# A decoder trunk on one core: the next pass's gather behind the scatter, a peeled last pass, and reordered norm, gate and down-projection steps

## The chip, the cores and the metric

The program runs on one core of one Trainium2 chip. The metric is the device time of one execution in microseconds, the lower the better. All arithmetic on the path is float32.

## What is computed

Two layers work on 256 tokens of 1024 channels. Each layer normalises x, makes one input projection, runs three token mixers (gated DeltaNet, RWKV-7, stick-breaking attention), merges them by sigmoid gates, projects and adds to x. Then a second norm and a channel mixer follow, and a last norm ends the trunk. Cut to what matters here:

```python
for layer in range(DEPTH):                       # DEPTH = 2
    hn = rmsnorm(x, norm_mix_g[layer])
    proj = hn @ w_in[layer]
    ...                                          # three mixers, gates = sigmoid(h_gate)
    x = x + merged @ w_out[layer]
    hn = rmsnorm(x, norm_ffn_g[layer])
    if layer % 2 == 0: x = x + (silu(hn @ w_gate) * (hn @ w_up)) @ w_down      # 2816 hidden
    else:              x = x + moe_swiglu(hn, ...)        # top 2 of 8 experts, 3584 hidden
return rmsnorm(x, final_norm_g)
```

## The kernel before

Everything is written by hand, engine by engine: TensorE (PE), ScalarE (ACT), VectorE (DVE), GpSimd (POOL) and the queue of SyncE (SP) each have their own list of instructions, and semaphores (the `Signal` objects and plain `sem`) tie them. The order on each engine is the order in which its functions are called. The 256 tokens are two tiles of 128 (`t` = 0, 1). Weights come through a ring of slots that SP fills in the order of the `loads` list; SP waits for the release of a slot before it issues the load that follows into it.

**Norm at the start of a layer** (`scaled` L1622, `turned` L1627, called at L2037 to L2044; PE's `first_projections` L644). ACT squares a tile and makes 1/rms, DVE's `scaled` writes hn, PE transposes it, DVE's `turned` multiplies the transposed tile by the norm's weights into hnT. PE's first projections read hnT of tile 0 (L636).

**Attention** (PE L1010 to L1059, DVE L1860 to L1879, ACT's `log1p` L1524, POOL's masks L571 to L580). Eight heads go in four pairs `j`. PE makes the scores of the next pair, then some steps of other work, then the suffix sums of the pair (`sums`, L1034 and L1035), other steps, then `values` (L1045, L1048). The other steps are the first six gate projections (`gate_projections`, L623, two matmuls a step, eight steps for a gate); twelve of the 48 steps have run before attention. Two PSUM banks, `proj`, take these projections in turn, so the first matmul of gate m waits until DVE has copied gate m-2 out of its bank (`opened`, L1873, the copy is L1876). `opens` says behind which pair DVE makes which copy:

```python
opens = ((), (0, 1), (2,), (3,))
```

**Dense channel mixer of layer 0** (`dense_ffn` L1095, DVE's L1907). For each of 22 tiles of hidden channels PE makes gate and up (L1144), and one tile later the down projection (L1104), for both token tiles. The down projections of the last three tiles are kept and run token tile by token tile. DVE then adds to x (L1915), tile 0 first, and waits for both tiles before it goes on to the next layer's norm.

**Experts of layer 1** (`experts` on PE L1212, DVE L2008, ACT L1580 to L1596, SP L2145 to L2171). Tokens are sorted into passes of up to 80 slots, one expert for a pass; here 8 passes run. Each pass has four rounds; a round takes 11 MB of weights, in eight slots for gate and up and three for down. At the end of a pass PE does, in this order: `gather(i + 1)` (selection matrix times hn, L1190 with operand hn, into B[0] and B[1]), eight transposes of the pass's result (L1292), the scatter back to tokens (L1299, into B[0], B[1], proj[0], proj[1]), and `selection_rows(i + 1)` (L1207, into B[0]). ACT copies yT (L1592) and ye (L1596) between them; DVE copies the gathered tokens (`gathered`, L2000), adds the four scatter blocks to x (L2032) and copies the selection rows (L2006). The last pass does the same, though nothing follows it. Each of these loops runs a number of times that is read from a table.

**Final norm** (ACT L1598 to L1603, DVE L2053 to L2057, SP L2171 to L2174). After the loop DVE signals once (`all_added`); ACT squares both tiles and makes both 1/rms values; DVE multiplies each tile by 1/rms and the norm's weights in one SCALAR_TENSOR_TENSOR; SP stores each tile when it is done.

## Time and profile before

| | |
|---|---|
| median of 3 runs | 2057.37 us (2057.05 to 2058.26) |
| the profiled execution | 2054.16 us |
| its span, first to last instruction | 2052.4 us |
| PE busy | 1962.2 us, 96% |
| DVE, ACT, POOL busy | 392.6, 271.1, 88.2 us |
| granted TensorE clock, mean | 0.984 of full speed |
| DMA | 482.92 MB, 235 GB/s over the span |

The span leaves out what lies before the first and behind the last instruction (1.8 us of the execution's own 2054.16). PE busy counts a matmul as busy also where it runs at the lower clock. A line number names the line of the kernel; many operations of different stages share a helper's line, so stretches of time tell the stages apart. The stages of layer 0 end near 695 us, the experts begin near 1177 us.

### The profile page before, as it was taken

The numbers are of one execution on the slowest core, as the hardware profiler recorded it, in microseconds if no ns is written. First come the engines' busy times: TensorE is split into PE (matmuls) and PEld (weight loads), VectorE is DVE, ScalarE is ACT, GpSimd is POOL, SyncE is SP. The second block draws the span as 40 slices with busy tenths as digits, with TensorE's granted clock in tenths as the row PEclk, the third lists the DMA queues.
The fourth block names the chain that finished last, engine by engine and source line by source line (L and its number), as shares of the span: only waits on it lengthen the run. The fifth ranks groups of instructions, "written<-read, shape, count | busy, mean of one in ns | idle before, by whom it ended". The sixth has DMA issues, their size and how long they took to land.

```text
span 2052.4 us, 66808 instructions
## 1 busy us (share of the span) xinstructions
PE 1962.2 (96%) x31214; PEld 1742.7 (85%) x31214; DVE 392.6 (19%) x948; ACT 271.1 (13%) x579; POOL 88.2 (4%) x174
## 2 busy tenths in 40 slices
PE   7999999999999999999999799999999999999997
PEld 7888887888777788888788799999999898989896
DVE  3335331110000133533211300101000101010001
ACT  1223223000000122222320000000000000000001
POOL 4011101000000001011000000000000000000000
PEclk9999999999999999999999899999999999999999
DMA  7313123467442151311345389999999999999996
GB/s 239 123 44 102 43 84 103 144 207 244 144 144 82 42 160 47 101 45 43 107 139 204 137 335 407 407 407 407 407 407 407 407 407 407 407 407 407 407 407 240
DMA packets 214760, 482.92 MB, mean 235 GB/s; under 512 B 11582, under 2 KB 110092, under 8 KB 214668
## 3 DMA queue, kind: packets, MB, share of 16 engines
q1 hardware_dynamic: 214668, 481.54, 62.9%
q8 instruction: 77, 1.26, 0.3%
q14 instruction: 15, 0.12, 0.0%
HBM read 480.46 MB, written 1.05 MB: 235 GB/s over the span
## 4 chain that ended last, share of the span: by engine, by line
PE 83%; DMA 6%; SPq 4%; DVE 3%; ACT 1%; issue 1%; POOL 0%; DVEq 0%; POOLq 0%
PE bank L1190 29%; PE bank L623 18%; PE bank L1144 7%; DMA pool<-in_moe_w_down_dram 6%; PE bank L713 5%; PE bank L1071 4%; PE bank L1104 4%; SPq L2111 3%; PE bank L1087 3%; PE bank L636 2%; PE bank L677 2%; PE bank L1299 1%; SPq L2116 1%; PE bank L1034 1%; DVE pool L1814 0%
## 5 line engine op out<-in xcount | busy, mean ns | idle before, releaser
L1190 PE MATMUL bank<-pool 128*64 128x80 f32 x21504 | 759.5, 234 | 32.1 <-DMA pool<-in_moe_w_down_dram 23.5
L1190 PEld LDWEIGHTS bank<-pool 128*64 128x64 f32 x21504 | 752.6, 138 | 40.3 <-DMA pool<-in_moe_w_down_dram 25.8
L623 PE MATMUL bank<-hnT,pool 128*128 128x256 f32 x1856 | 431.5, 386 | 6.4 <-DVE pool L1876 6.4
L623 PEld LDWEIGHTS bank<-hnT,pool 128*128 128x128 f32 x1856 | 349.0, 192 | 61.7 <-issue 14.4
L1144 PEld LDWEIGHTS bank<-hnT,pool 128*128 128x128 f32 x640 | 121.6, 190 | 24.6 <-issue 9.1
L1144 PE MATMUL bank<-hnT,pool 128*128 128x256 f32 x640 | 141.2, 379 | 0.0
L2019 DVE TENSOR_TENSOR pool<-pool,bank 128x320 f32<-128x320 f32 x32 | 15.6, 488 | 637.4 <-ACT pool L1584 637.4
L713 PEld LDWEIGHTS bank<-pool 64*64 64x64 f32 x3008 | 94.8, 135 | 17.2 <-issue 11.3
L713 PE MATMUL bank<-pool 64*64 64x32 f32 (+2 forms) x3008 | 103.4, 221 | 2.6 <-DVE pool L1660 1.6
L1584 ACT ACTIVATE pool<-bank 128x320 f32<-128x320 f32 x32 | 14.0, 437 | 675.5 <-PE bank L1190 675.5
L561 POOL TENSOR_TENSOR pool<-pool,level_mask 128x256 f32<-128x256 f32 x72 | 51.9, 736 | 782.1 <-DVE pool L1736 502.1
L1071 PE MATMUL bank<-oT,pool 128*128 128x256 f32 x384 | 85.4, 380 | 0.0
L1071 PEld LDWEIGHTS bank<-oT,pool 128*128 128x128 f32 x384 | 72.8, 190 | 10.2 <-issue 0.3
L1104 PE MATMUL bank<-pool 128*128 128x512 f32 x176 | 78.8, 592 | 0.0
L1104 PEld LDWEIGHTS bank<-pool 128*128 128x128 f32 x176 | 33.4, 190 | 33.5 <-issue 27.7
L1087 PE MATMUL bank<-pool 128*128 128x256 f32 x256 | 55.9, 379 | 0.0
L1087 PEld LDWEIGHTS bank<-pool 128*128 128x128 f32 x256 | 48.5, 190 | 6.5
L636 PE MATMUL bank<-hnT,pool 128*128 128x128 f32 x384 | 47.9, 290 | 4.6 <-DVE hnT L1631 4.6
L636 PEld LDWEIGHTS bank<-hnT,pool 128*128 128x128 f32 x384 | 47.3, 206 | 5.1 <-issue 5.0
L1910 DVE TENSOR_TENSOR pool<-pool,bank 128x256 f32<-128x256 f32 x22 | 9.3, 421 | 204.8 <-ACT pool L1562 204.8
L1660 DVE TENSOR_TENSOR pool<-pool,bank 128x128 f32<-128x128 f32 x108 | 26.7, 285 | 92.5 <-PE bank L713 92.5
L1562 ACT ACTIVATE pool<-bank 128x256 f32<-128x256 f32 x22 | 8.4, 383 | 206.8 <-PE bank L1144 195.7
(323 smaller groups left out, 1222.4 us busy)
## 6 DMA issues: line engine op xcount, KB each, us to landing
pool<-in_moe_w_up_dram SPq DMA_DIRECT2D x128, 896.0 KB, 16.6
pool<-in_moe_w_gate_dram SPq DMA_DIRECT2D x128, 896.0 KB, 16.6
pool<-in_w_in_dram SPq DMA_DIRECT2D x66, 1024.0 KB, 5.3
pool<-in_moe_w_down_dram SPq DMA_DIRECT2D x64, 1024.0 KB, 16.8
pool<-in_moe_w_down_dram SPq DMA_DIRECT2D x32, 1536.0 KB, 18.6
pool<-in_ffn_w_gate_dram SPq DMA_DIRECT2D x11, 1024.0 KB, 8.5
pool<-in_ffn_w_up_dram SPq DMA_DIRECT2D x11, 1024.0 KB, 5.7
pool<-in_ffn_w_down_dram SPq DMA_DIRECT2D x11, 1024.0 KB, 5.1
```

Of the source, the lines that this page charges most:

```text
L561: ml_ready.by(gp.tensor_tensor(Ml[:, 4 * g:4 * g + 4, :], m_of(g), rep(level_mask[:, b, :], 4), ALU.mult))
L623: ins = mm(ps[:, s * T:(s + 1) * T], w[:, k, (j + s) * P:(j + s + 1) * P], hnT[:, k, :], start=(k == 0), stop=(k == KD - 1))
L636: ins = mm(ps[:, s * T + t * P:s * T + (t + 1) * P], w(s, k), hnT[:, k, t * P:(t + 1) * P], start=(k == 0), stop=(k == KD - 1))
L677: ins = mm(ps[:, half * SW:(half + 1) * SW], hnT[:, k, t * P:(t + 1) * P], weights(n)[:, k, :], start=(k == 0), stop=(k == KD - 1))
L713: ins = mm(out(rows), lhs(rows), rhs(rows), start=True, stop=True, skip_group_check=True)
L1071: ins = mm(ps[:, s * T:(s + 1) * T], weights(n)[:, k, (j0 + s) * P:(j0 + s + 1) * P], oT[:, m // 4, k, :], start=(k == 0), stop=(k == GH - 1))
L1087: ins = mm(bank[:, s * SW:(s + 1) * SW], mT[:, k, t * P:(t + 1) * P], weights(n)[:, k, :], start=(k == 0), stop=(k == KD - 1))
L1104: ins = mm(B[2 * t + half][:, :], ffT[:, f, t * P:(t + 1) * P], weights(n)[:, i, half * 512:half * 512 + 512], start=(f == 0), stop=(f == ...
L1144: ins = mm(proj[f % 2][:, s * T:(s + 1) * T], w[:, k, i * P:(i + 1) * P], hnT[:, k, :], start=(k == 0), stop=(k == KD - 1))
L1190: ins = mm(bank[rows, cs], w[:, rows], rhs, start=start, stop=stop, skip_group_check=True)
L1660: ins = tt(old, old, part(B[2 + g][:, k * T:(k + 1) * T]), ALU.subtract)
L2111: sp_.dma_start(hidden_slot(n), src).then_inc(hid_loaded[n], 16)
```

## The change

1. **Order at the end of a pass.** PE now transposes and scatters at once, makes the selection rows (into B[2]) and only then gathers for the next pass, once the first two of the four adds are done. DVE adds first, then copies the selection rows, then the gathered tokens.
2. **Last pass of DVE on its own.** DVE's loop runs one time less, and the last pass is written out behind it, without selection rows and `gathered`, with a signal for each token tile (`all_added` 1 and 2).
3. **Final norm by halves.** ACT squares tile 0 while DVE still adds tile 1. DVE multiplies x by the norm's weights alone (into `xf`), without waiting for the statistics. Then ACT scales tile 0 (`Copy` with a scale) and DVE tile 1, and each is stored. `xf` and `xs` lie over weight slots that are no longer used.
4. **Norm at the start of a layer.** DVE turns tile 0 before it scales tile 1.
5. **Attention.** Four steps instead of five between `sums` and `values`; DVE copies gate 0 behind the first pair and gate 1 behind the second.
6. **Dense mixer.** Six kept down projections instead of three.

```diff
@@ attention, PE @@
                     some(steps, 5)
                     sums(2 * j)
                     sums(2 * j + 1)
-                    some(steps, 5)
+                    some(steps, 4)
                     values(j)
@@ dense_ffn, PE @@
-                        if f - 1 >= LAST - 2:
+                        if f - 1 >= LAST - 5:
                             kept.append(former)
@@ selection_rows, PE @@
-                    ins = pe.transpose(B[0][0:CAP, t * P:(t + 1) * P], selw[:, t, :], ident[:])
+                    ins = pe.transpose(B[2][0:CAP, t * P:(t + 1) * P], selw[:, t, :], ident[:])
@@ experts, PE, end of a pass @@
-                    pe.wait_ge(sc_added, i * 4 + 4)
-                    gather(i + 1)
-
                     for half in range(2):
                         pe.wait_ge(yT_ready, i * 2 + (half + 1))
                         for k in range(4):
                             ins = pe.transpose(B[2 + half][0:CAP, k * P:(k + 1) * P], yT[:, 4 * half + k, :], ident[:])
                         ins.then_inc(ye_mm, 1)
-                    pe.wait_ge(xg_ready, i * 2 + 4)
                     for half in range(2):
...
-                    pe.wait_ge(sc_added, i * 4 + 5)
                     selection_rows(i + 1)
+                    pe.wait_ge(sc_added, i * 4 + 6)
+                    gather(i + 1)
@@ final norm, ACT @@
-            act.wait_ge(all_added, 1)
             for t in range(NT):
-                ins = A(hn[:, t, :], x[:, t, :], ACT.Square, accum_out=stat[:, 32 + t:33 + t])
+                act.wait_ge(all_added, t + 1)
+                ins = A(xs[:, t, :], x[:, t, :], ACT.Square, accum_out=stat[:, 32 + t:33 + t])
             link(ins)
             link(A(stat[:, 34:36], stat[:, 32:34], ACT.Ln, scale=1.0 / D, bias=eps_c[:, 0:1]))
             A(stat[:, 36:38], stat[:, 34:36], ACT.Exp, scale=-0.5).then_inc(frms_ready, 1)
+            act.wait_ge(frms_ready, 1)
+            act.wait_ge(xf_ready, 2)
+            A(xf[:, 0, :], xf[:, 0, :], ACT.Copy, scale=stat[:, 36:37]).then_inc(fin0_ready, 1)
@@ attention, DVE @@
-                opens = ((), (0, 1), (2,), (3,))
+                opens = ((0,), (1,), (2,), (3,))
@@ experts, DVE @@
-                with v.Fori(0, n_pass) as i:
+                def one_pass(i, last):
...
-                    gathered(i + 1)
                     for half in range(2):
                         for t in range(NT):
...
-                            ins.then_inc(sc_added, 1)
-                    selection_rows(i + 1)
+                            ins.then_inc(all_added if last and half else sc_added, 1)
+                    if not last:
+                        selection_rows(i + 1)
+                        gathered(i + 1)
+
+                with v.Fori(0, more) as i:
+                    one_pass(i, False)
+                one_pass(more, True)
@@ start of a layer and final norm, DVE @@
+                v.wait_ge(vec_ready, l + 1)
+                turned(l, 0, 0)
                 scaled(l, 0, 1)
-                v.wait_ge(vec_ready, l + 1)
-                for t in range(NT):
-                    turned(l, 0, t)
+                turned(l, 0, 1)
...
-            v.memset(rs[:, 60:61], 0.0).then_inc(all_added, 1)
-            v.wait_ge(frms_ready, 1)
             v.wait_ge(fgain_loaded, 16)
             for t in range(NT):
-                stt(x[:, t, :], x[:, t, :], stat[:, 36 + t:37 + t], fgain, ALU.mult, ALU.mult).then_inc(fin_ready, 1)
+                v.wait_ge(all_added, t + 1)
+                ins = tt(xf[:, t, :], x[:, t, :], fgain, ALU.mult)
+            ins.then_inc(xf_ready, 1)
+            v.wait_ge(xf_ready, 2)
+            v.wait_ge(frms_ready, 1)
+            ts(xf[:, 1, :], xf[:, 1, :], stat[:, 37:38], None, ALU.mult).then_inc(fin_ready, 1)
```

The order on DVE in attention, before. L1867 is a head's softplus step, L1876 the copy of a gate out of its bank (`bank` is PSUM, `pool` the large SBUF tensor):

```order
L1867 SCALAR_TENSOR_TENSOR pool<-bank,pool 128x384 [waits l1_ready] x4
L1876 COPY pool<-bank 128x512 [waits proj_mm] x2
L1867 SCALAR_TENSOR_TENSOR pool<-bank,pool 128x384 [waits loga_mm,l1_ready] x2
L1876 COPY pool<-bank 128x512 [waits proj_mm]
L1867 SCALAR_TENSOR_TENSOR pool<-bank,pool 128x384 [waits loga_mm,l1_ready] x2
```

And of the changed kernel (the same two lines are L1870 and L1879 there):

```order
L1870 SCALAR_TENSOR_TENSOR pool<-bank,pool 128x384 [waits l1_ready] x2
L1879 COPY pool<-bank 128x512 [waits proj_mm]
L1870 SCALAR_TENSOR_TENSOR pool<-bank,pool 128x384 [waits l1_ready] x2
L1879 COPY pool<-bank 128x512 [waits proj_mm]
L1870 SCALAR_TENSOR_TENSOR pool<-bank,pool 128x384 [waits loga_mm,l1_ready] x2
```

The first copy moved from behind four softplus steps to behind two.

The order on PE at the end of a pass, of the changed kernel (L1292 transposes, L1298 the scatter, L1210 the selection rows, L1193 with operand hn the gather):

```order
L1292 MATMUL bank<-ident,pool 80x128 [waits yT_ready]
L1298 MATMUL bank<-hnT,pool 128x512 [waits ye_ready]
L1210 MATMUL bank<-ident,pool 80x128 x2
L1198 REGISTER_ALU [waits sc_added]
L1193 MATMUL bank<-pool,hn 64x80 [waits sel_ready]
```

Before, the 32 matmuls of the gather stood ahead of the first of these rows, and the scatter also waited for `xg_ready`.

## Rows read from the trace of the kernel before

**Rows 1.** Stretches of the experts: us, PE, PEld, DVE, ACT, POOL, PEclk, DMA share, GB/s
```profile
1187.00:1214.00 27.00, 23.84 (x669) 23.31 (x666) 0.89 (x2) 0.81 (x2) 0.00 (x0) 1.00 0.96 359
...
1889.00:1916.00 27.00, 24.03 (x680) 23.53 (x678) 0.89 (x2) 0.85 (x3) 0.00 (x0) 1.00 1.03 407
```
**Rows 2.** PE's waits over the whole span: us in total, times, longest us
```profile
PE bank L1190 <- DMA pool<-in_moe_w_down_dram: 23.5, 14, 2.1
...
PE bank L623 <- DVE pool L1876: 6.4, 2, 3.2
```
**Rows 3.** Timeline, attention of layer 1, first pair: start us, us, engine, instruction
```profile
998.77 0.56 DVE L1867 SCALAR_TENSOR_TENSOR pool<-bank,pool 128x384 f32<-128x384 f32 x1 [0.93 <-ACT pool L1531]
...
1002.22 1.28 DVE L1876 COPY pool<-bank 128x512 f32<-128x512 f32 x2
...
1003.05 1.85 PE L623 MATMUL bank<-hnT,pool 128*128 128x256 f32 x4 [3.19 <-DVE pool L1876]
...
1007.40 4.48 PE L623 MATMUL bank<-hnT,pool 128*128 128x256 f32 x20
```
**Rows 4.** The same stretch in microseconds, columns as in rows 1
```profile
1004.00:1005.00 1.00, 1.00 (x4) 0.82 (x3) 0.00 (x0) 0.00 (x0) 0.00 (x0) 0.50 0.29 111
```
**Rows 5.** Timeline, attention of layer 1, last pair, PE
```profile
1037.06 4.58 PE L623 MATMUL bank<-hnT,pool 128*128 128x256 f32 x20
...
1043.21 1.03 PE L623 MATMUL bank<-hnT,pool 128*128 128x256 f32 x4
...
1044.52 0.65 PE L1045 MATMUL bank<-pool 128*64 128x256 f32 x4 [0.28 <-POOL pool L579]
```
**Rows 6.** Timeline, start of layer 1, DVE and PE
```profile
697.01 0.75 DVE L1625 TENSOR_SCALAR hn<-x,stat 128x1024 f32<-128x1024 f32 x1
...
699.04 0.27 DVE L2039 COPY vecs<-bank 128x103 f32<-128x103 f32 x1 [1.28 <-PE bank L1308]
...
699.89 1.28 DVE L1631 TENSOR_TENSOR hnT<-bank,vecs 128x512 f32<-128x512 f32 x2
...
701.31 6.18 PE L636 MATMUL bank<-hnT,pool 128*128 128x128 f32 x32 [2.31 <-DVE hnT L1631]
```
**Rows 7.** Timeline, start of layer 0, PE
```profile
13.60 5.33 PE L636 MATMUL bank<-hnT,pool 128*128 128x128 f32 x32 [2.32 <-DVE hnT L1631]
```
**Rows 8.** Timeline, end of the dense mixer: DVE's last adds
```profile
695.69 1.28 DVE L1915 TENSOR_TENSOR x<-x,bank 128x512 f32<-128x512 f32 x2 [3.87 <-PE bank L1104]
```
**Rows 9.** Timeline, PE: the very first gather, then the first pass's end and the next's start
```profile
1177.08 4.18 PE L1190 MATMUL bank<-pool,hn 128*64 128x80 f32 x64 [5.20 <-DVE pool L1988]
...
1280.04 2.39 PE L1190 MATMUL bank<-pool,hn 128*64 128x80 f32 x64
...
1288.99 11.22 PE L1190 MATMUL bank<-pool 128*64 128x80 f32 x318
```
**Rows 10.** Timeline from the end of the last pass on, all engines
```profile
2035.47 2.38 PE L1190 MATMUL bank<-pool,hn 128*64 128x80 f32 x64
2035.69 0.44 ACT L1592 ACTIVATE pool<-bank 128x320 f32<-128x320 f32 x1 [1.22 <-PE bank L1190]
...
2038.45 1.07 ACT L1596 ACTIVATE hnT<-bank 80x512 f32<-80x512 f32 x2 [2.33 <-PE bank L1292]
...
2039.19 3.67 PE L1299 MATMUL bank<-hnT,pool 80*128 80x512 f32 x8 [0.34 <-ACT hnT L1596]
...
2042.90 0.69 DVE L2032 TENSOR_TENSOR x<-x,bank 128x512 f32<-128x512 f32 x1 [0.17 <-PE bank L1299]
...
2043.98 1.06 ACT L1600 ACTIVATE hn<-x 128x1024 f32<-128x1024 f32 x1 [3.15 <-DVE pool L2053]
...
2046.76 2.48 DVE L2057 SCALAR_TENSOR_TENSOR x<-x,stat,hnT 128x1024 f32<-128x1024 f32 x2 [2.83 <-ACT stat L1603]
...
2049.27 0.36 SPq L2174 DMA_DIRECT2D out_dram<-x  x1
```
**Rows 11.** DMA issues of that stretch: KB each, median us to landing
```profile
out_dram<-x SPq DMA_DIRECT2D x2, 512.0 KB, 2.7
```

More of the change, by code:

```diff
@@ L220, in build @@
         top[0] = MRING * SLOT
+        xf = pool[:, 0:NT * D].rearrange("p (t n) -> p t n", t=NT)
+        xs = pool[:, NT * D:2 * NT * D].rearrange("p (t n) -> p t n", t=NT)
         xgT = region(KD * CAP).rearrange("p (k n) -> p k n", k=KD)
@@ L448, in build @@
         marg_exp = sem("marg_exp")
+        fin0_ready, xf_ready = marg_exp, oneh_ready
         def over(ap, n):
@@ L1911, in dense_ffn @@
                 for t in range(NT):
-                    down_mm.wait(v, 0, down_mm.per_layer - 2 * (1 - t))
+                    down_mm.wait(v, 0, down_mm.per_layer - 3 * (1 - t))
                     for half in range(2):
@@ L2005, in selection_rows @@
                 v.wait_ge(selT_mm, i + 1)
-                v.tensor_copy(selwT[0:CAP, :], B[0][0:CAP, 0:T]).then_inc(selT_ready, 1)
+                v.tensor_copy(selwT[0:CAP, :], B[2][0:CAP, 0:T]).then_inc(selT_ready, 1)
             def experts():
@@ L2012, in experts @@
                 pass_table()
-                n_pass = v.value_load(pass_expert[0:1, 0:1], min_val=MIN_PASSES, max_val=MAX_PASSES)
+                more = v.value_load(pass_expert[0:1, MAX_PASSES + 1:MAX_PASSES + 2], min_val=MIN_PASSES - 1,
+                                    max_val=MAX_PASSES - 1)
                 gathered(0)
                 selection_rows(0)
-                with v.Fori(0, n_pass) as i:
+                def one_pass(i, last):
                     for r in range(NR):
@@ L2170, in _ @@
             rest_of_pass(more, e)
-            sp_.wait_ge(fin_ready, 1)
-            sp_.dma_start(out[0, 0:P, :], x[:, 0, :]).then_inc(out_stored, 16)
-            sp_.wait_ge(fin_ready, 2)
-            sp_.dma_start(out[0, P:T, :], x[:, 1, :]).then_inc(out_stored, 16)
+            for t in range(NT):
+                sp_.wait_ge(*((fin0_ready, 2), (fin_ready, 1))[t])
+                sp_.dma_start(out[0, t * P:(t + 1) * P, :], xf[:, t, :]).then_inc(out_stored, 16)
             sp_.wait_ge(out_stored, 32)
```

## The prediction

> **What bounds the kernel now.** I read the stretches of the expert stage first, then PE's waits over the whole span, then the timeline around each place that the change touches.
>
> The expert stage is bound by the weight stream, not by PE. From 1187 us on the DMA engines are full, and 27 us late in the stage move 407 GB/s with a share of 1.03 while PE is idle for 3 of them [rows 1]. PE waits 23.5 us for weights of the down projection alone [rows 2], 2.9 us for each of the 8 passes. So from about 1187 us to the landing of the last weights nothing that PE saves between passes can show, and nothing that it loses below some 2.9 us a pass. What can shorten the run lies ahead of that stream (its later loads follow PE's progress, so it starts earlier by what PE gains before it) and behind it (the tail).
>
> Ahead of it PE is the bound, and the rows show where it stands still. The largest wait inside a stage is 6.4 us in 2 pieces, 3.2 us in each layer, for DVE's copy L1876 [rows 2]. In attention of layer 1, for example, PE has done four of its five steps, and the fifth needs the bank of gate 0. DVE could copy that bank when its second softplus step is over, started at 998.77 us, but it does two more of these, which wait for ACT, and copies at 1002.22 us [rows 3].
>
> **Attention (item 5), both layers.** The copy now starts where the second L1867 step ends, some 0.5 us after 998.77 (in rows 3 one follows the other without a gap), at 999.24 us. From the start of a copy to PE's matmul it was 1003.05 - 1002.22 = 0.83 us, so PE goes on at 1000.07 us instead of 1003.05: **2.98 us**. DVE's third softplus step waits for ACT anyway, 0.93 us in the row of the second [rows 3], more than the copy's 0.64 us (half of 1.28), so nothing behind it moves.
>
> The wait has a second price. Behind it the granted clock is 0.50 [rows 4], the lower level of 1.2 GHz. From the late matmul to the next filler, 4 records and the sums, took 1007.40 - 1003.05 = 4.35 us [rows 3]. In the last pair 20 records and the same sums took 1043.21 - 1037.06 = 6.15 us at 2.4 GHz; 16 records fewer at 4.48 / 20 = 0.22 us make 2.6 us [rows 5]. With a wait of 0.2 us in place of 3.2 I take the clock to stay up: **1.75 us** more. If it falls all the same, this term is 0, the other bound.
>
> The last pair had one step ahead of `values` and PE waited 0.28 us there for POOL [rows 5]; now it has four: **0.28 us**. The first three pairs lose one step each, 0.87 us of cover (four records), between sums and values. I bound what that costs by the last pair: with a single step of cover the wait was 0.28 us, so with four steps it is nothing. The 48 steps are the same work. One layer: 2.98 + 1.75 + 0.28 = 5.0 us, two layers **10.0 us** (6.5 if the clock does not follow).
>
> **Start of a layer (item 4).** In layer 1 DVE's copy of the vectors ends at 699.31 us, `scaled` of tile 1 runs, and `turned` of tile 0 starts at 699.89 us; PE, idle for 2.31 us, starts at 701.31 us [rows 6]. Without `scaled` in between `turned` starts at about 699.37: **0.52 us**. Layer 0 has the same pattern, PE idle 2.32 us and started at 13.60 us [rows 7]; the same 0.5 us. `scaled` of tile 1 is needed only when PE's first 32 records, 6.18 and 5.33 us, are over. Both 32 run slower than the 96 behind them would; if the clock rises no earlier than before, half of the gain stays, if it no longer falls in layer 1 up to 2.5 us come on top. I take **1.0 us** for both, bounds 0.5 and 3.5.
>
> **Dense mixer (item 6).** Six kept projections let tile 0's sums end 12 records earlier. But DVE adds tile 1 at 695.69 us, after PE's last matmul, and only behind both adds does it scale tile 0, at 697.01 us [rows 8, 6]. That pair of adds is unmoved, so the earlier tile 0 waits for it: 0. PE's work is the same, only reordered; the last down slot is released as many matmuls before the end as before. 0 on both sides.
>
> **End of a pass (items 1, 2), passes 1 to 7.** Before, PE's last weight matmul ended where the gather starts, 1280.04 us, and the next pass began at 1288.99, 8.95 us later [rows 9]. Now the transposes wait for ACT's copy of yT but not for the gather. Taken over from the tail below, the scatter starts 2.3 us earlier, and so do the adds and the selection rows. The gather, 2.39 us, starts behind them at about 1285.35, its second half is copied by DVE at 1288.3, and the next pass begins at about 1288.9. The same within 0.2 us, and under the stream's cover of 2.9 us a pass. 0. Without that cover it would be 7 x 0.1 us.
>
> **Tail (items 1 to 3).** Last weight matmul 2035.47 us, ACT's second copy of yT ends at 2035.69 + 0.44 = 2036.13 [rows 10]. The eight transposes no longer stand behind 2.38 us of gather. ACT's copy of ye, at 2038.45 before, starts at about 2036.15, right behind its copy of yT: 2.3 us earlier, and so are scatter and adds. The third add ended at 2042.90 - 0.17 = 2042.73, now at 2040.4; ACT squares tile 0 from there instead of from 2043.98, that is at 2040.5, 3.5 us earlier. Its two squares and the statistics keep their 2.78 us (2043.98 to 2046.76): 2043.3. DVE's fourth add ends at 2043.59 - 2.3 = 2041.3; two multiplications by the weights, priced as L2057, 1.24 us each, end at 2043.8, so they are late now, not the statistics. DVE's scale is L1625's form, 0.75 us [rows 6]; ACT's scale of 1024 columns is priced by its square, 1.06 us [rows 10]: it ends at 2044.9. The stores go out at 2045.0 and 2045.4 instead of the second at 2049.27. Landing takes 2.7 us [rows 11], but 512 KB take 1.3 us at 407 GB/s and both stores now run at once, so the second lands at 2048.1 to 2049.0. Against 2049.27 + 2.7 = 2051.97 before that is 3.0 to 3.9 us: I take **3.5 us**. The peeled code adds none: the loop's last pass had the same instructions and its front waits for PE.
>
> One rule speaks against this part. The scatter of the last pass, right behind eight transposes, took 3.67 us for 8 records of 512 columns [rows 10], 0.46 us each, as at the upper clock; the transposes did not bring it down. The Trainium skill ("TensorE: Matmul & The Clock Gate", Part 4: PE-mode transpose) says that transposes don't count as activity for the clock the way other matmuls do. By it the changed tail, where no gather stands ahead of them any more, would scatter at the half clock, and by that the tail would give some 3 us less.
>
> **The sum.** 10.0 + 1.0 + 3.5 = 14.5 us. The profiled execution, 2054.16 us, becomes 2039.7; it lies 3.2 us under the median of the three runs, and against the median, 2057.37, I forecast **2042.9 us**, 0.7% less.
>
> **Rivals.**
> 1. *The clock does not follow.* The half clock comes behind the shortened wait too, or moves to the tail behind a late wait for weights. For it: it fell behind each long wait. Against it: 0.2 us is no such wait. 2042.9 + 3.5 = 2046.4 us.
> 2. *The expert stream swallows what is gained ahead of it.* If the stream's end were set by something other than its start, only the tail would count: 2057.4 - 3.5 = 2053.9 us. Against it: at 1187 to 1214 us it moved 359 GB/s and PE took part in its pace [rows 1]; it can't have begun sooner than PE's first rounds.
> 3. *The change of order slows every pass.* One mechanism: the end of a pass runs at 1.2 GHz, because PE now waits for ACT, transposes, waits for ACT and only then does dense work. The gather did run that slowly once, 4.18 us instead of 2.39 [rows 9]: 1.8 us. The scatter would double, 3.4 us more, and the next pass's first matmuls would cost the 1.75 us of attention: 6.95 us a pass. Above the 2.9 us of cover that is 7 x 4.05 = 28.4 us, and 3.4 us in the tail: 2042.9 + 31.8 = 2074.7 us, slower. It decides from a growth of about 2.9 + (14.5 + 4.1) / 7 = 5.6 us a pass, less than that is hidden or paid by the other terms. Against it: the scatter of rows 10.
> 4. *The clock at layer 1's start no longer falls.* 2042.9 - 2.5 = 2040.4 us.
>
> **How the numbers follow.** Forecast 0.78, rival 1 0.11, rival 4 0.04, rival 2 0.04, rival 3 0.03. A measurement of this kernel tells about 0.2%, 4.1 us, from no change, so rival 2 at 2053.9 is "the same" and all but rivals 2 and 3 are faster: 0.93, 0.04, 0.03. The range takes in rivals 1 and 4 and the bounds of the tail (1.5 us less): 2039.5 to 2048.0 us.
>
> **What would show it.** PE's waits: L626 for L1879 with some 0.4 us in all instead of 6.4, no wait for POOL ahead of `values`, granted clock 1.0 through the first pair. The start of layers: idle ahead of L639 of 1.8 us instead of 2.3. The expert stretches: again 407 GB/s throughout, gather behind the scatter, about 9 us between the last and the first weight matmul, everything about 11 us earlier. The tail: from the last weight matmul to the end of the span 13.4 us instead of 16.9, with DVE's multiplications the last to be ready. Wrong would be: a DMA rate under 400 GB/s around a pass's end, a wait for ACT or POOL in attention that was not there, or a stream that starts earlier and ends at the same time.

## The result

| | before | after |
|---|---|---|
| median (range) of the runs compared, us | 2057.21 (2054.36 to 2058.26, 4 runs) | 2040.39 (2039.24 to 2042.13, 4 runs) |
| ratio, with its 95% interval | | 0.9921 (0.9904 to 0.9938) |
| the profiled execution, us | 2054.16 | 2039.24 |
| its span, us | 2052.4 | 2037.5 |

The change is faster by 0.8%, and 2040.39 us lies inside the predicted range (2039.5 to 2048.0), 2.5 us below the forecast of 2042.9. Span against span it is 14.9 us, where the sum was 14.5. The rest of the distance is the profiled executions' place in their scatter: the one before lay 3.2 us under the median that the prediction started from, the one after 1.2 us under its own.

The first matmuls of the stages, read from PE's timeline of both kernels, tell where it went. A line named in the table stands 3 lines lower in the changed kernel (L705 is L708 there).

| from, to | before, us | after, us | difference |
|---|---|---|---|
| layer 0: first transpose (L705) to first use of L800 | 87.89 | 89.93 | +2.0 |
| layer 0: to attention (L1026) | 209.49 | 209.49 | 0 |
| layer 0: attention, to the first merge (L1071) | 50.70 | 45.69 | -5.0 |
| layer 0: merge and dense mixer, to layer 1's first transpose | 342.67 | 342.68 | 0 |
| layer 1: first transpose to first use of L800 | 87.33 | 84.42 | -2.9 |
| layer 1: to attention | 209.48 | 209.50 | 0 |
| layer 1: attention | 50.70 | 45.69 | -5.0 |
| layer 1: merge and routing, to the first gather | 131.75 | 131.76 | 0 |
| experts: to the matmul on the last down weights | 850.59 | 849.75 | -0.8 |
| from there to the end of the span | 24.7 | 21.5 | -3.2 |

PE's waits over the whole span after (us in total, times, longest us):

```profile
PE bank L1193 <- DMA pool<-in_moe_w_down_dram: 24.1, 14, 2.1
...
PE bank L1193 <- DMA pool<-in_moe_w_up_dram: 5.4, 6, 0.9
...
PE bank L1225 <- DVE pool L2003: 4.7, 7, 0.7
PE bank L639 <- DVE hnT L1634: 3.5, 2, 1.8
PE bank L1193 <- issue: 2.9, 4, 1.3
...
PE bank L626 <- DVE pool L1879: 0.4, 2, 0.2
```

The wait for the copy went from 6.4 us in 2 pieces [rows 2] to 0.4; the wait for weights of the down projection, 24.1 us, is nearly what it was (23.5). The first pair of attention in layer 1, timeline after (start us, us, engine, instruction):

```profile
992.90 0.56 DVE L1870 SCALAR_TENSOR_TENSOR pool<-bank,pool 128x384 f32<-128x384 f32 x1 [0.93 <-ACT pool L1531]
993.37 0.68 DVE L1879 COPY pool<-bank 128x512 f32<-128x512 f32 x1
994.38 0.56 DVE L1870 SCALAR_TENSOR_TENSOR pool<-bank,pool 128x384 f32<-128x384 f32 x1 [0.33 <-ACT pool L1531]
...
994.20 1.10 PE L626 MATMUL bank<-hnT,pool 128*128 128x256 f32 x4 [0.22 <-DVE pool L1879]
...
996.87 3.40 PE L626 MATMUL bank<-hnT,pool 128*128 128x256 f32 x15
```

Other than in [rows 3], DVE copies between its second and its third softplus step. The third still waits for ACT behind the copy, and PE stands still for 0.22 us in place of 3.19. The four late records take 1.10 us in place of 1.85. From them to the next filler it is 996.87 - 994.20 = 2.67 us where it was 4.35. The granted clock in that stretch answers [rows 4] (columns as in rows 1), and is 1.00 where it was 0.50; the experts answer [rows 1], the same 407 GB/s:

```profile
994.00:995.00 1.00, 0.80 (x4) 0.75 (x5) 0.61 (x2) 0.97 (x3) 0.00 (x0) 1.00 0.00 0
995.00:996.00 1.00, 1.00 (x6) 0.71 (x5) 0.12 (x1) 0.81 (x2) 0.41 (x1) 1.00 0.75 123
...
1176.00:1203.00 27.00, 24.05 (x675) 23.52 (x671) 0.89 (x2) 0.81 (x2) 0.00 (x0) 1.00 0.95 359
1878.00:1905.00 27.00, 23.96 (x678) 23.45 (x676) 0.89 (x2) 0.81 (x2) 0.00 (x0) 1.00 1.03 407
```

PE's timeline at the start of layer 1 and at the end of the first pass, after; they answer [rows 6] and [rows 9]:

```profile
694.83 1.09 PE L708 MATMUL bank<-ident,hn 128*128 128x128 f32 x8 [2.17 <-DVE hn L1628]
...
697.78 5.44 PE L639 MATMUL bank<-hnT,pool 128*128 128x128 f32 x32 [1.77 <-DVE hnT L1634]
...
1261.78 6.82 PE L1193 MATMUL bank<-pool 128*64 128x80 f32 x192
1268.53 1.24 PE L1292 MATMUL bank<-ident,pool 128*80 128x128 f32 x8
1269.84 3.70 PE L1298 MATMUL bank<-hnT,pool 80*128 80x512 f32 x8
1273.38 0.38 PE L1210 MATMUL bank<-ident,pool 128*80 128x128 f32 x2
1273.69 2.44 PE L1193 MATMUL bank<-pool,hn 128*64 128x80 f32 x64
...
1277.28 4.92 PE L1193 MATMUL bank<-pool 128*64 128x80 f32 x136
```

The wait ahead of the first projections is 0.54 us shorter; the 2.17 us ahead of the transposes stand as before. The pass's end has the new order, and from its last to the next weight matmul it is 1277.28 - 1268.60 = 8.7 us, where it was 8.95.

The tail, all engines, after; it answers [rows 10]:

```profile
2023.84 1.24 PE L1292 MATMUL bank<-ident,pool 128*80 128x128 f32 x8
...
2024.52 1.20 ACT L1596 ACTIVATE hnT<-bank 80x512 f32<-80x512 f32 x2
2025.16 3.70 PE L1298 MATMUL bank<-hnT,pool 80*128 80x512 f32 x8
...
2028.76 1.06 ACT L1600 ACTIVATE pool<-x 128x1024 f32<-128x1024 f32 x1 [1.75 <-DVE x L2035]
...
2029.51 2.35 DVE L2065 TENSOR_TENSOR pool<-x,hnT 128x1024 f32<-128x1024 f32 x2
...
2031.96 1.15 ACT L1606 ACTIVATE pool<-pool,stat 128x1024 f32<-128x1024 f32 x1 [0.44 <-DVE pool L2065]
2033.13 0.84 SPq L2185 DMA_DIRECT2D out_dram<-pool  x2
```

ACT's copy of ye starts 0.68 us after the last weight matmul (2.98 before), ACT's scale waits for DVE's multiplications as foreseen, and both stores are issued 9.3 us after that matmul. The scatter takes 3.70 us right behind the transposes.

### The profile page after: what moved, and what is told of

The parts are those of the page before. It is cut to its first block, busy times and chain, and to the rows that moved or that the text cites. A ratio compares the mean times of both kernels' runs of the same rounds, so it can differ in the third digit from the quotient of the medians.

```text
span 2037.5 us, 66780 instructions
## 1 busy us (share of the span) xinstructions
PE 1961.5 (96%) x31214; PEld 1740.2 (85%) x31214; DVE 392.2 (19%) x945; ACT 273.1 (13%) x580; POOL 88.0 (4%) x174
## 3 DMA queue, kind: packets, MB, share of 16 engines
q8 instruction: 77, 1.26, 0.3%
HBM read 480.46 MB, written 1.05 MB: 236 GB/s over the span
## 4 chain that ended last, share of the span: by engine, by line
PE 84%; DMA 6%; SPq 4%; DVE 3%; issue 1%; ACT 1%; POOL 0%; DVEq 0%; ACTq 0%
PE bank L1193 29%; PE bank L626 19%; PE bank L1147 7%; DMA pool<-in_moe_w_down_dram 6%; PE bank L716 5%; PE bank L1074 4%; PE bank L1107 4%; SPq L2123 3%; PE bank L1090 3%; PE bank L639 2%; PE bank L680 2%; PE bank L1298 1%; SPq L2128 1%; PE bank L1037 1%; DVE pool L1817 0%
## 5 line engine op out<-in xcount | busy, mean ns | idle before, releaser
L1193 PE MATMUL bank<-pool 128*64 128x80 f32 x21504 | 759.3, 234 | 32.8 <-DMA pool<-in_moe_w_down_dram 24.1
L1193 PEld LDWEIGHTS bank<-pool 128*64 128x64 f32 x21504 | 752.6, 138 | 40.9 <-DMA pool<-in_moe_w_down_dram 26.3
L626 PE MATMUL bank<-hnT,pool 128*128 128x256 f32 x1856 | 431.5, 386 | 0.4 <-DVE pool L1879 0.4
L626 PEld LDWEIGHTS bank<-hnT,pool 128*128 128x128 f32 x1856 | 349.2, 192 | 55.9 <-issue 8.5
L1147 PEld LDWEIGHTS bank<-hnT,pool 128*128 128x128 f32 x640 | 121.6, 190 | 23.4 <-issue 7.6
L639 PE MATMUL bank<-hnT,pool 128*128 128x128 f32 x384 | 48.5, 292 | 3.5 <-DVE hnT L1634 3.5
L639 PEld LDWEIGHTS bank<-hnT,pool 128*128 128x128 f32 x384 | 47.9, 208 | 4.0 <-issue 4.0
L2035 DVE TENSOR_TENSOR x<-x,bank 128x512 f32<-128x512 f32 x32 | 22.0, 688 | 97.9 <-PE bank L1298 97.9
## 6 DMA issues: line engine op xcount, KB each, us to landing
pool<-in_moe_w_down_dram SPq DMA_DIRECT2D x64, 1024.0 KB, 16.8
```

The costliest lines, as they stand in the source:

```text
L626: ins = mm(ps[:, s * T:(s + 1) * T], w[:, k, (j + s) * P:(j + s + 1) * P], hnT[:, k, :], start=(k == 0), stop=(k == KD - 1))
L639: ins = mm(ps[:, s * T + t * P:s * T + (t + 1) * P], w(s, k), hnT[:, k, t * P:(t + 1) * P], start=(k == 0), stop=(k == KD - 1))
L1147: ins = mm(proj[f % 2][:, s * T:(s + 1) * T], w[:, k, i * P:(i + 1) * P], hnT[:, k, :], start=(k == 0), stop=(k == KD - 1))
L1193: ins = mm(bank[rows, cs], w[:, rows], rhs, start=start, stop=stop, skip_group_check=True)
```

## The experiments

Twelve more runs follow, one of them the changed kernel again. Each is given by its difference from the kernel before or from the changed kernel. Times are compared by their ratio to the kernel before, run beside them, with a 95% interval.

### Attention: copies or steps

**a1_attention**: the kernel before with item 5 alone.

```diff
-                    some(steps, 5)      # between sums and values
+                    some(steps, 4)
...
-                opens = ((), (0, 1), (2,), (3,))
+                opens = ((0,), (1,), (2,), (3,))
```

> The kernel before with the change of attention alone: the copy of gate 0's bank at the first place and four steps in place of five ahead of `values`. My theory: each layer gets back the wait of 3.0 us, the half-clock stretch of 1.75 us and the wait for POOL of 0.3 us, so the time is 10.0 us less than before (0.9951), L1071's first matmul comes 5.0 us sooner after L1026's first in each layer, and the wait for the copy falls from 6.4 us in 2 pieces to 0.4. Rival 1, the clock does not follow: 6.5 us less (0.9968). Rival 2, the expert stream swallows what is gained ahead of it: 0.

Measured: 0.9951 (0.9936 to 0.9966), and attention of both layers 45.70 us in place of 50.70. The wait:

```profile
PE bank L623 <- DVE pool L1876: 0.4, 2, 0.2
```

The first gather comes 8.6 us earlier and the matmul on the last down weights (2017.85 us) 9.8 us earlier than before, so the expert stage passes on all that is gained ahead of it: rival 2 is out. (Of the 10.0 us, 2.2 went at the layers' starts, of which below, and 0.7 came back between merge and gather.) 5.0 us a layer is more than the 3.2 us of the wait, so rival 1 is out too.

**a2_copies_only**: the second hunk of that diff alone. (The expectation's "after the first softplus step" is not what ran: the copy stands behind the first pair's two steps, as in the changed kernel.)

> The kernel before with the table of copies alone changed (gate 0's bank copied after the first softplus step, each later bank one pair of heads apart); five steps stay ahead of `values` after the first three pairs, one after the last. My theory: the copy is what PE waited for, so 3.0 + 1.75 us a layer come back, 9.5 us in all (0.9954); the wait for POOL ahead of the last `values`, some 0.3 us a layer, stays. Rival: the number of steps is what does it, and the earlier copy alone gives nothing or leaves a part of the 3.2 us wait: 0 to 3 us less.

Measured: 0.9953 (0.9938 to 0.9969), attention 46.04 us. The copies give 4.66 us a layer, and what is left against a1, 0.34 us, is the wait ahead of the last `values`:

```profile
PE bank L1045 <- POOL pool L579: 0.6, 2, 0.3
```

**b1_steps_only**: the first hunk alone.

> The kernel before with four steps ahead of every `values` and the copies at their old places. My theory: the wait of 3.2 us a layer for the copy stays, since the fifth step of the first pair stands ahead of the sums; the wait for POOL ahead of the last `values` goes, so attention is 0.3 us shorter in each layer (50.7 to 50.4), the time 0.6 us less. Rival: the first three pairs lose cover and wait for POOL, and attention gets longer.

Measured: one execution of 2055.67 us, too few for a ratio; attention 50.35 us in both layers, and the wait of 6.4 us in 2 pieces unchanged:

```profile
PE bank L623 <- DVE pool L1876: 6.4, 2, 3.2
```

The two halves of item 5 add up: 4.66 + 0.35 = 5.01. The first three pairs, one step poorer each, pay nothing for it.

### The start of a layer

**a3_norm_and_kept**: the kernel before with items 4 and 6.

```diff
                 v.wait_ge(vec_ready, l + 1)
-                for t in range(NT):
-                    turned(l, 0, t)
+                turned(l, 0, 0)
+                scaled(l, 0, 1)
+                turned(l, 0, 1)
...
-                        if f - 1 >= LAST - 2:
+                        if f - 1 >= LAST - 5:
```

> The kernel before with items 4 and 6 alone: `turned` of tile 0 ahead of `scaled` of tile 1, and six kept down projections in place of three. My theory: 0.5 us a layer from the norms' order, PE's idle time ahead of L636 at the start of layer 1 1.8 us in place of 2.3; the kept projections nothing, since DVE's scale of tile 0 still stands behind its second pair of adds, so that the gap ahead of the transposes at layer 1's start stays at 2.2 us. In all 1.0 us less, with up to 2 us of scatter either way by where the granted clock falls to 0.50 in the stretches behind the starts. Rival: the kept projections free tile 0 earlier, so the gap of 2.2 us is gone: 3 us less.

Measured: 0.9991 (0.9981 to 1.0), by that ratio 1.9 us less, with an interval that just reaches no change. PE and DVE at layer 1's start:

```profile
696.72 1.29 DVE L1915 TENSOR_TENSOR x<-x,bank 128x512 f32<-128x512 f32 x2 [9.01 <-PE bank L1104]
698.04 0.75 DVE L1625 TENSOR_SCALAR hn<-x,stat 128x1024 f32<-128x1024 f32 x1
...
698.84 1.43 PE L705 MATMUL bank<-ident,hn 128*128 128x128 f32 x8 [2.17 <-DVE hn L1625]
...
702.21 4.18 PE L636 MATMUL bank<-hnT,pool 128*128 128x128 f32 x18 [1.77 <-DVE hnT L1631]
```

Tile 0 is added at 686.41 us, 10 us earlier than tile 1, and then lies there: DVE waits 9.01 us for tile 1 before it scales anything. So the gap of 2.17 us stays, the kept projections give nothing, and the norms' order gives the 0.5 us.

**d1_changed_again**: the changed kernel once more.

> The changed kernel once more, unaltered, to tell what differs from one execution to the next: my theory is that attention (45.7 us), L800 to L1026 (209.5), the tail (21.5 us from the last down weights) and the passes repeat within 0.1 us, and that the stretches at a layer's start (L705 to L768, L768 to L800), where the granted clock falls, differ by 1.6 us and more. Rival: they repeat too, and the 1.3 us gained at layer 1's start belong to the norms' order.

Measured: 2040.25 us (2039.62 to 2043.84), ratio 0.9927 (0.9909 to 0.9944). Attention took 45.69 us and L800 to L1026 209.48, as expected. The tail missed the expectation: from the last down weights to the end of the span it took 2038.4 - 2015.23 = 23.2 us and not 21.5, since the 224 matmul records behind that wait took 9.61 us in place of 7.97 (the granted clock was 0.54 at 2015.2 to 2018 us). From the end of the last weight matmul on both traces took 13.59 us. The layers' starts, which I expected to differ, repeated, 89.86 and 84.42 us where the first trace has 89.93 and 84.42, which speaks for the rival. Other runs speak against it, since five of them (b3 and c1 to c4 below) have the same instructions as the changed kernel ahead of the experts:

| first transpose to first use of L800, us | layer 0 | layer 1 |
|---|---|---|
| old order of the norm: before, a1, a2, a4, b1 | 87.9, 89.9, 90.9, 91.6, 90.4 | 87.3, 87.5, 87.9, 87.5, 87.4 |
| new order: after, d1, b3, c1, c2, c3, c4 | 89.9, 89.9, 89.2, 89.5, 89.3, 87.2, 89.1 | 84.4, 84.4, 87.2, 87.6, 87.2, 88.4, 87.3 |
| new order on the old kernel: a3 | 89.2 | 86.8 |

The same instructions take 84.4 to 88.4 us in layer 1, and the piece from L768 to L800 takes 15.3, 16.9 or 18.5 us and nothing between. So most of the -2.9 of the table in the result, and the +2.0 of layer 0, lie within what one code varies by. The means of the rows, 90.1 to 89.2 in layer 0 and 87.5 to 86.7 in layer 1, put item 4 at 0.9 us a layer, hardly to be told from 0.5 within such scatter.

**b4_start_in_dense**: the changed kernel, and layer 1's norm of tile 0 moved into the dense mixer's last 10 us, which the six kept projections open.

```diff
@@ dense_ffn, PE, kept projections of tile 1 @@
                             down_done(n, i, ins)
+                            if f == LAST - 2:
+                                transposes_of_hn(1, 0, 0)
+                                ff_ready.wait(pe, 0, LAST + 1)
+                                vectors(1)
@@ first_projections(1), PE @@
-                transposes_of_hn(l, 0, 0)
-                vectors(l)
...
-                half_tokens(ps1, column(n1), 0)
+                    half_tokens(ps1, column(n1), 0, (0,))
+                    transposes_of_hn(l, 0, 1)
+                    half_tokens(ps1, column(n1), 0, (1,))
@@ dense_ffn, DVE @@
                     fx_ready.by(ins)
+                    if t == 0:
+                        scaled(1, 0, 0)
+                        copied(1)
+                        turned(1, 0, 0)
```

(`copied` is DVE's wait for and copy of the vectors; DVE does the three no more at layer 1's start.)

> The changed kernel and one thing more: with six kept down projections tile 0 is done 10 us before the dense mixer ends, so DVE scales it right behind its first pair of adds, and PE turns it and the vectors between the last kept projections of tile 1; layer 1 then begins with the first projection, and tile 1 is turned halfway through the second. My theory: PE's gaps at layer 1's start (2.2 us ahead of the transposes, 1.8 us ahead of L639's like) are gone, and if the granted clock stays at 1.00 there, the first 32 records take 3.7 us in place of 5.4: 5.7 us less than the changed kernel, some 0.9894 of before; 4.0 us less if the clock falls all the same. Rival: DVE's copy and turns now stand ahead of its adds of tile 1, or tile 1 is late for PE, and a new wait of 2 us or more takes the place of the old gaps: 0 to 2 us less.

Measured: 2033.13 us (2032.69 to 2033.37), ratio 0.9896 (0.9879 to 0.9912). Its slowest run lies 5.9 us below the fastest of the changed kernel's eight (2039.24 us). Against the kernel before, run beside each, the ratios (0.9896, and 0.9921 and 0.9927 for the changed kernel) give 5 to 6 us, the medians 7. It is the fastest version of this study. PE's timeline there:

```profile
688.50 1.04 PE L715 MATMUL bank<-ident,hn 128*128 128x128 f32 x8
...
689.47 3.62 PE L1114 MATMUL bank<-pool 128*128 128x512 f32 x8
692.92 5.52 PE L639 MATMUL bank<-hnT,pool 128*128 128x128 f32 x48
698.28 1.04 PE L715 MATMUL bank<-ident,hn 128*128 128x128 f32 x8
699.15 9.10 PE L639 MATMUL bank<-hnT,pool 128*128 128x128 f32 x80
```

No row has a wait, and 48 records take 5.52 us where 32 took 5.44: both gaps and the half clock behind them are gone. From the first merge of layer 0 to L768 of layer 1 it took 404.2 us, against 411.8 to 414.2 in the seven traces of the changed kernel's code. That is at least 7.7 us where 5.7 were expected. In the nearest of them (411.8), 1.6 of the 2.0 us beyond the expectation is a second half-clock stretch, from 745 to 749 us, in and behind which 76 records of L626 took 18.21 us in place of 16.65; b4 has none there.

### The end of a pass and the tail

**a4_pass_and_tail**: the changed kernel with items 4, 5 and 6 as before.

```diff
-                    some(steps, 4)      # between sums and values
+                    some(steps, 5)
...
-                        if f - 1 >= LAST - 5:
+                        if f - 1 >= LAST - 2:
...
-                opens = ((0,), (1,), (2,), (3,))
+                opens = ((), (0, 1), (2,), (3,))
...
-                turned(l, 0, 0)
                 scaled(l, 0, 1)
-                turned(l, 0, 1)
+                v.wait_ge(vec_ready, l + 1)
+                for t in range(NT):
+                    turned(l, 0, t)
```

> The changed kernel with attention, the norms' order and the kept projections as before: the order at a pass's end and the tail remain. My theory: the passes hide their order under the weight stream (the down weights are waited for 23 to 24 us as before, 407 GB/s around each pass's end), and the tail gives 3.2 to 3.5 us (0.9984), from the last weight matmul to the span's end 13.5 us in place of 16.9. Rival: PE's order in the passes also moves the stream, by 0.3 us a pass or more either way: 1 us less or 5.5 us less.

Measured: 0.9986 (0.9976 to 0.9995), 2.9 us less. From the last down weights to the end of the span 2052.7 - 2031.11 = 21.6 us, as in the changed kernel; weights of the down projection are waited for 25.2 us. From the first gather to the last down weights it took 850.3 us, 850.6 before. The rival's moved stream isn't there: ten traces without added work, of either order, lie between 849.0 and 850.6 us.

**b3_gather_first**: the changed kernel with the gather ahead of the transposes again, and `gathered` ahead of DVE's adds.

```diff
@@ experts, PE, end of a pass @@
+                    pe.wait_ge(sc_added, i * 4 + 4)
+                    gather(i + 1)
                     for half in range(2):
...
+                    pe.wait_ge(xg_ready, i * 2 + 4)
                     for half in range(2):
...
                     selection_rows(i + 1)
-                    pe.wait_ge(sc_added, i * 4 + 6)
-                    gather(i + 1)
```

> The changed kernel with the gather of the next pass ahead of the transposes again, for DVE ahead of the adds too; the transposes of the selection rows keep their new bank, the final norm by halves stays. My theory: in the passes nothing, down weights are waited for 22 to 25 us as in both kernels; in the tail the gather's 2.3 us stand on the path again, so 2.3 us more than the changed kernel (0.9932 of before in place of 0.9921), and the final norm by halves keeps only some 1 us of the tail's 3.2. Rival: the norm by halves and the peeled pass made the whole tail gain, and the gather's place is worth nothing: equal to the changed kernel.

Measured: 0.9940 (0.9923 to 0.9956), 2043.32 us; 0.9932 was expected, which the interval takes in. From the last down weights to the end 2041.3 - 2017.45 = 23.85 us, 2.3 more than after, and 23.4 us of waiting for down weights:

```profile
2017.45 7.97 PE L1193 MATMUL bank<-pool 128*64 128x80 f32 x224 [2.13 <-DMA pool<-in_moe_w_down_dram]
...
2025.25 2.38 PE L1193 MATMUL bank<-pool,hn 128*64 128x80 f32 x64
```

So of the tail's 3.2 us the gather's place gives 2.3 and the norm by halves 0.9, and in the passes the place is worth nothing.

**c1_one_more_gather** and **c2_four_more_gathers**: how much does the weight stream cover at a pass's end?

```diff
                     pe.wait_ge(sc_added, i * 4 + 6)
+                    for _ in range(1):      # 4 in c2
+                        gather(i + 1, signal=False)
                     gather(i + 1)
```

> The changed kernel with one more gather (its result overwritten by the next) between the selection rows and the gather of each pass's end: 2.4 us more work of PE in each of 8 passes, 7 of them ahead of more weights. My theory: PE waits 2.9 us a pass for down weights, so 2.4 us vanish there: the time as the changed kernel's within 1 us, the waits for down weights 17 us shorter. Rival 1, PE's pass end is on the path: 16.8 us more. Rival 2, part of the cover comes too late in the pass or loads follow PE's releases: some us more.

> The changed kernel with four more gathers at each pass's end, 9.6 us of PE. My theory: 3.0 us a pass are covered by the wait for down weights, the rest is paid: 7 x 6.6 = 46 us more than the changed kernel, and no wait for down weights in the passes is left. Rival 1, no cover: 67 us more. Rival 2, the weight stream runs on its own and its buffers take up more than that: under 25 us more.

Measured: 2124.51 us (ratio 1.0340) and 2148.82 us (1.0458), that is 84 and 108 us more than the changed kernel. Every theory on record missed both: the most that any gave was 16.8 us for c1 and 67 for c2. PE's waits and the queue of instructions of c1:

```profile
PE bank L1193 <- issue: 47.4, 33, 3.8
PE bank L1225 <- issue: 39.7, 7, 5.8
```

```profile
q8 instruction: 141, 2.31, 0.5%
```

The same queue (packets, MB, share of 16 engines) of the changed kernel:

```profile
q8 instruction: 77, 1.26, 0.3%
```

PE no longer waits for weights; it waits for its own instructions, and 64 more packets of instructions are read, 1.05 MB. My reading: with the 64 matmul records of one more gather PE's loop over the passes reads its code from memory again each of the seven times that it goes round, some 9 packets a time. Before and after it does not: both kernels have 77 packets, and their `issue` waits on weight matmuls (2.9 us in 4 pieces after) all lie in the first pass. The waits of c1 are 47.4 + 39.7 - 2.9 - 4.7 = 79.5 us more. The seven added gathers ahead of weights, 2.2 us each, make some 15 us, and the changed kernel's 29.5 us of waiting for weights are gone. That leaves some 18 of the 84 us, which I did not measure apart. Behind the stalls the clock is low; two stretches of c1 at the start of the second pass (columns as in rows 1):

```profile
1288.00:1292.00 4.00, 1.84 (x15) 1.09 (x15) 0.00 (x0) 0.00 (x0) 0.00 (x0) 0.50 0.85 336
1292.00:1296.00 4.00, 2.71 (x40) 2.71 (x42) 0.00 (x0) 0.00 (x0) 0.00 (x0) 0.50 0.05 17
```

The Trainium skill ("Runtime: NRT & Kernel Launch", Instruction fetch mechanics) gives PE 128 KiB for instructions, refilled in blocks of 16 KiB, and says that a branch to code that isn't there stalls. The size of the packets agrees, 1.05 MB / 64 = 16.4 KB. It also calls the crossing of a block mostly hidden; the stalls of up to 3.8 us inside a pass of c1 are not. So c1 and c2 do not answer the question about the cover. That the reread code is their cause rests on the packets and on the `issue` waits; the loop was not made shorter elsewhere to see it go, so this is not shown.

**c3_three_reductions** and **c4_nine_reductions** ask it again with PE's code as it was: DVE holds up the next pass, at seven pass ends.

```diff
                         selection_rows(i + 1)
+                        for c in range(3):      # 9 in c4
+                            v.tensor_reduce(B[3][:, c:c + 1], hn[:, 0, :], AX_X, ALU.max)
                         gathered(i + 1)
```

> The changed kernel with three reductions of 1024 columns on DVE (1.22 us each where the kernel has one such, result unused) ahead of its two multiplications that release the next pass: PE's code is unchanged, only its wait at the pass's end grows, by 2.6 us. My theory: the wait for down weights, 2.9 us a pass, covers it: the changed kernel's time within 1 us, the waits for down weights shorter by 7 x 2.6 = 18 us and PE's wait for xg_ready (L1225) longer by as much; what the extra gather cost before was PE's code, read from memory again in each pass, not the time at the pass's end. Rival: the pass's end itself is on the path: 18 us more, and with some loss of the stream's rate as with the extra gather up to 80.

> The changed kernel with nine such reductions, 9.9 us more at each of 7 pass ends. My theory: 3.0 us a pass are covered, 7 x 6.9 = 48 us are paid. Rival 1, no cover: 69 us. Rival 2, the stream's buffers cover more than PE's waits show: under 30 us.

Measured: c3 2040.04 us (ratio 0.9921), the changed kernel's time. Its waits:

```profile
PE bank L1225 <- DVE pool L2003: 19.5, 7, 2.8
PE bank L1193 <- DMA pool<-in_moe_w_down_dram: 12.4, 7, 2.1
...
PE bank L1193 <- DMA pool<-in_moe_w_up_dram: 1.8, 2, 0.9
```

14.8 us more in front of the passes (2.1 a pass, where I expected 2.6), 15.3 us less for weights: one is paid out of the other. c4 took 2075.78 us (1.0095), 35.5 us more than the changed kernel, and has this wait and no row for weights:

```profile
PE bank L1225 <- DVE pool L2003: 66.8, 7, 9.5
```

62.1 us more of waiting, 35.5 paid, so 26.6 us were covered, 3.8 us a pass and not 3.0. The cover is the waits for down and up weights together, 24.1 + 5.4 = 29.5 us: 62.1 - 29.5 = 32.6, and the last 2.9 us may be the half clock behind each long wait (0.50 at 1286 to 1290 us). I did not measure that apart, and the changed kernel has such stretches too, behind waits for weights (the 224 records of its second pass took 9.59 us, those of its last 7.97). c4 missed both its figures, my 48 us and rival 2's under 30: mine counted the down weights alone and took 9.9 us of delay a pass where it was 8.9.

## Why the prediction was right

**What bounds the kernel.** As put: only what lies ahead of the stream and behind it counts. a1 shows the first (8.6 us at the first gather, all of it still there at the end), a4 and b3 the second, c3 that 2.1 us more at every pass's end cost nothing. The size of the cover was off. The prediction spread the 23.5 us of rows 2 over 8 passes, 2.9 us each, but all 14 waits lie in the last seven, 3.4 us each, and the waits for up weights (5.3 us before) belong to it: 4.1 us a pass by the rows, 3.8 by c4. Nothing of the forecast hung on that. Rival 3's threshold of 5.6 us a pass would be some 6.5.

**Attention, 10.0 us**: 5.0 us in each layer. The wait, the half clock and the wait for POOL all came out as worked out; PE goes on 0.83 us after the copy's start, as before, and the clock stays at its upper level (2.4 GHz, granted 1.00). Rival 1 did not happen.

**Start of a layer, 1.0 us**: the waits ahead of L639 are 1.77 us in both layers (2.32 and 2.31 before), the 0.5 us each. What the clock makes of it varies by more than the term: layer 0's first 32 records took 6.65 us after and 5.33 before. No run here separates 1.0 from the mean of 1.8. Layer 1's 32 records still run slower (5.44 us), so rival 4 did not happen here; b4 shows what it takes, both gaps away.

**Dense mixer, 0**: right, and for the reason given, DVE's unmoved second pair of adds (a3).

**Pass ends, 0**: 8.7 us between the weight matmuls (8.9 predicted), 405 to 409 GB/s around the first pass's end, and b3 with the old order waits for weights as long. Rival 3 did not happen: the next gather takes 2.44 us behind the scatter (2.39 before), the upper level.

**Tail, 3.5 us**: 3.2 in the trace. The steps up to the stores hold within 0.3 us: multiplications done 8.0 us after the last weight matmul (8.3 predicted), ACT's scale 9.3 (9.4). The part that was mis-sized is the landing: from the first store's issue to the end of the span 2037.5 - 2033.13 = 4.4 us, where I had 3.1 to 4.0 (2045.0 to 2048.1 or 2049.0), with a median landing of 3.1 us for two stores at once against 2.7 [rows 11]. Behind the transposes the granted clock was 1.00, and the scatters of all eight passes took 29.6 us, 3.70 each, the upper level. The prediction set a page against this part (the Trainium skill, "TensorE: Matmul & The Clock Gate", Part 4), which says that transposes don't count as activity for the clock as other matmuls do, and took from it 3 us less. That did not happen; whether transposes count, these eight, 1.24 us in all, don't tell.

The three parts measured alone give 0.49 + 0.14 + 0.09 = 0.72%, the whole 0.79 and 0.73%, so no gain or loss by their combination shows.

**What was luck.** Attention and the tail, 13.2 of the 14.9 us, repeat from trace to trace. The other 1.7 us come from +2.0 and -2.9 at the layers' starts, where one code varies by up to 4 us, and -0.8 in the experts, where traces without added work vary by 1.6. That they come out near the sum's 1.0 us is chance; so is that the two profiled executions lay where they did in their scatter, which is most of the 2.5 us between forecast and median.

## What to carry to other kernels

Read PE's long waits together with the clock behind them: a wait of 3.2 us for one copy cost 4.7, and moving that copy ahead of one pair's steps in another engine's list, where that engine waited anyway, gave it all back. An earlier result is worth nothing as long as its consumer's list has something later ahead of it (six kept projections alone: 0 us; with the norm moved up behind them: 5 to 7 us). The cover of the experts was near the sum of all waits for weights, not the largest row alone. And before adding instructions to a long hardware loop, compare the instruction queue's packets of both traces: work of 2.2 us a pass, about what c3 shows to be hidden, cost 84 us, by the counters because the loop's code was read again.

## What the runs showed of the hardware that was not expected

**Code that is read again.** 77 packets and 1.26 MB of instructions in both kernels, 141 and 2.31 MB with one gather more in PE's loop, 149 and 2.44 MB with four. The stalls of the first were up to 5.8 us at the top of a pass and 3.8 us within.

**The clock falls without a wait.** PE's stretch from L768 to L800 begins with 40 matmuls of one to eight columns and has no pause, and the granted clock falls there to 0.50 in both kernels. When it falls and rises differs from one execution to the next: two stretches around it in layer 0, of before and then of after (columns as in rows 1):

```profile
84.00:86.00 2.00, 2.00 (x17) 2.00 (x17) 1.17 (x9) 0.66 (x4) 0.00 (x0) 0.77 0.00 0
...
88.00:90.00 2.00, 2.00 (x9) 1.69 (x9) 0.00 (x0) 0.00 (x0) 0.00 (x0) 0.88 0.00 0
```

```profile
84.00:86.00 2.00, 2.00 (x11) 2.00 (x11) 0.00 (x0) 0.23 (x2) 0.00 (x0) 0.50 0.00 0
...
88.00:90.00 2.00, 2.00 (x9) 1.82 (x8) 0.22 (x1) 0.00 (x0) 0.00 (x0) 0.50 0.00 0
```

That piece took 15.3, 16.9 or 18.5 us, steps of 1.6 us, and d1's last down projection differs by as much (9.61 and 7.97 us). The changed kernel's eight times differ by 4.6 us; how much of that is made of such steps no run shows, but two single profiles can differ by one or more of them for no other reason.
